# mLSTM heads with tokens on partitions: denominators as a column of the values product, norm and gate inside the heads' block

## What is computed

```python
def mlstm_mixer(h, w_in, gate_b, head_g, w_out):
    q, k, v, ig, fg, og = jnp.split(h @ w_in, splits, axis=-1)
    hh = mlstm_chunkwise(heads(q), heads(k), heads(v), i_pre, f_pre)
    hh = rmsnorm(hh.transpose(0, 2, 1, 3), head_g).reshape(B_, S, A_V_W)
    return (hh * jax.nn.sigmoid(og)) @ w_out
# inside mlstm_chunkwise, for a token t and a head:
#   s[t, u] = (q_t . k_u) * 64**-0.5 * exp(log_d[t, u] - m_t) for u <= t
#   h_t     = sum_u s[t, u] v_u / max(|sum_u s[t, u]|, exp(-m_t))
```

## Time and profile before

| | us |
|---|---|
| median of 3 runs | 3057.55 |
| lowest, highest | 3047.7, 3060.89 |
| the profiled execution, its own time | 3049.9 |
| its span in the profile | 3048.1 |
| mean granted clock of TensorE | 0.961 |
| busy: TensorE, VectorE, ScalarE, GpSimd | 2815.7, 1561.3, 871.8, 376.5 |

### The profile page before, as it was taken

How to read it: one execution, slowest core, us unless ns; L and a number is a source line. 1 busy time by engine, 2 the same in 40 slices (tenths; PEclk the granted TensorE clock), 3 DMA queues, 4 the chain that set the end, 5 groups by cost and what they waited for, 6 DMA issues and landing times. The chain is left out here.

```text
span 3048.1 us, 40943 instructions
## 1 busy us (share of the span) xinstructions
PE 2815.7 (92%) x17635; PEld 2216.8 (73%) x17635; DVE 1561.3 (51%) x2138; ACT 871.8 (29%) x1119; POOL 376.5 (12%) x356
## 2 busy tenths in 40 slices
PE   7999999788899999999999999799999669999997
PEld 6888876577765777788887854578887545688886
DVE  5555454566676734555545317463354545463342
ACT  3222234211134223322213423332222334432221
...
DMA packets 267444, 272.05 MB, mean 89 GB/s; under 512 B 12751, under 2 KB 248246, under 8 KB 267071
## 3 DMA queue, kind: packets, MB, share of 16 engines
...
## 5 line engine op out<-in xcount | busy, mean ns | idle before, releaser
L915 DVE TENSOR_TENSOR mix_wl<-ring_raw,mix_wh 128x2048 fp32r<-128x2048 f32 (+2 forms) x66 | 153.1, 2320 | 220.1 <-ACT mix_wh L807 220.0
L707 PE MATMUL mix_ps<-h_mix_hi,mix_wh 128*128 128x512 f32 x624 | 244.1, 391 | 0.0
L709 PE MATMUL mix_ps<-h_mix_lo,mix_wh 128*128 128x512 f32 x624 | 242.8, 389 | 0.0
L807 ACT ACTIVATE mix_wh<-ring_raw 128x2048 fp32r<-128x2048 f32 (+2 forms) x66 | 117.6, 1782 | 212.5 <-PE mix_ps L713 162.1
L707 PE MATMUL ffn_ps<-h_rw_hi,ffn_wh 128*128 128x512 f32 x448 | 175.3, 391 | 0.0
L709 PE MATMUL ffn_ps<-h_rw_lo,ffn_wh 128*128 128x512 f32 x448 | 174.3, 389 | 0.0
L915 DVE TENSOR_TENSOR mlp_wl<-ring_raw,mlp_wh 128x2048 fp32r<-128x2048 f32 (+1 forms) x38 | 96.7, 2545 | 131.5 <-ACT mlp_wh L807 131.5
L915 DVE TENSOR_TENSOR mlp_wl<-mlp_raw,mlp_wh 128x2048 fp32r<-128x2048 f32 x36 | 93.2, 2589 | 133.3 <-ACT mlp_wh L807 133.3
L713 PE MATMUL mix_ps<-h_mix_hi,mix_wl 128*128 128x512 f32 x624 | 154.2, 389 | 0.0
L707 PE MATMUL mlp_ps<-view,mlp_wh 128*128 128x512 f32 x384 | 150.1, 391 | 0.0
L709 PE MATMUL mlp_ps<-view,mlp_wh 128*128 128x512 f32 x384 | 149.5, 389 | 0.0
...
## 6 DMA issues: line engine op xcount, KB each, us to landing
...
```

The lines of the kernel that those rows point to most:

```text
L707: nc.tensor.matmul(ps[:, it.banks[t], :], w(h, k, t), xh[:, k, :], start=it.first and k == it.k0, stop=False)
L709: nc.tensor.matmul(ps[:, it.banks[t], :], w(h, k, t), xl[:, k, :], start=False, stop=False)
L807: nc.scalar.activation(slot(wh, it), slot(raw, it), ACT.Copy).then_inc(hi_ready, 1)
L915: nc.vector.tensor_tensor(slot(wl, it), slot(raw, it), slot(wh, it).bitcast(F32), ALU.subtract)\
```

## The change

Tokens now lie on partitions in the product with the values. The pT block (keys by queries) is the stationary operand and the values of a head are the moving one, with a column of ones behind each head's 128 values, so that the 129th column of the result is the denominator. Ten products of 129 columns a head stand for the four of `pn` and the four of `pd`; `pd`, `pe_`, the mean and `den` are gone. `v` gets a layout with 129 columns a head (`padded_heads`), and the take-out of the values product of `mix` writes into it. The floors are turned once into columns (`fcol`) by four small transposes at the start.

Per head ScalarE copies the 4 by 129 columns out (`take_head`), squares each of the four blocks with a sum (`squares`), and VectorE works on 4 columns a head (`columns`: absolute value, floor, EPS d^2, sum). Reciprocal and root are taken in three groups of heads, (0,1,2), (3,4), (5,6,7); the roots of the first two groups stand inside the loop, after the exponential of unit (4,0) and of (6,0). VectorE then scales a head (`scale`), TensorE turns it back to features on partitions by four transposes into the one bank `pt` (`turn`), and VectorE multiplies by gain and gate out of PSUM (`gate`). Heads 0 to 4 are turned in the loop, after units (4,2), (5,0), (5,2), (6,2), (7,0); heads 5 to 7 after the last unit. `head_norm_gate` is removed, and with it its barrier. Each broadcast moves one unit earlier. Ten products of `keep_clock` are added before the first unit, four ahead of the wait for the constants and six behind the first scores.

The diff, cut:

```diff
+                        if st.padded:
+                            four = st.dst[:, t, TT * it.gi:TT * (it.gi + 1), 0:P]
+                            nc.scalar.activation(four, ps[:, t, :].rearrange("p (h n) -> p h n", n=P), ACT.Copy)\
+                                .then_inc(act_out, 1)
+                        else:
+                            nc.scalar.activation(st.dst[:, t, it.gi * L:(it.gi + 1) * L], ps[:, t, :], ACT.Copy)\
+                                .then_inc(act_out, 1)
...
+def padded_heads(e, at):
+    e.views += 1
+    return e.nc.alloc_sbuf_tensor_at(f"view{e.views}", [P, TT, A_HEADS, P + 1], F32, offset=e.arena_at + at * L * 4)[:, :, :, :]
...
+MH_GROUPS = ((0, 1, 2), (3, 4), (5, 6, 7))
+MH_ROOTS = {(4, 0): 0, (6, 0): 1}
+MH_TURNS = {(4, 2): 0, (5, 0): 1, (5, 2): 2, (6, 2): 3, (7, 0): 4}
...
+    H, W = A_HEADS, P + 1
+    group_of = {h: g for g, hs in enumerate(MH_GROUPS) for h in hs}
+    left = [h for h in range(H) if h not in MH_TURNS.values()]
-        negM, floor, den = sb("negM", [P, 3, L]), sb("floor", [P, 3, L]), sb("den", [P, 2, L])
-        sq = sb("sq", [P, 2, L])
-        pm, pe_, pS, pn, pd = (pb("pm", [P, L]), pb("pe", [P, L]), pb("pS", [P, 2, L]),
-                               pb("pn", [P, 2, L]), pb("pd", [P, 2, L]))
+        negM, sq = sb("negM", [P, 2, L]), sb("sq", [P, P])
+        outT = sb("outT", [P, H, TT, W])
+        fcol, mag = sb("fcol", [P, TT, H]), sb("mag", [P, 2, TT])
+        mean, rs = sb("mean", [P, H, TT]), sb("rs", [P, H, TT])
+        pm, pS, pn, pt = pb("pm", [P, L]), pb("pS", [P, 2, L]), pb("pn", [P, 2, 2, L]), pb("pt", [P, L])
...
+        def blocks_of(h):
+            return pn[:, h % 2, :, 0:2 * W].rearrange("p b (i n) -> p b i n", n=W)
...
             def broadcast(h):
                 if h > 0:
-                    pe.wait_ge(rows_out, 2 * h)
-                nc.tensor.matmul(pm[:, :], sel[:, h, :], rows[:, 0, :], start=True, stop=True)
-                nc.tensor.matmul(pe_[:, :], sel[:, h, :], rows[:, 1, :], start=True, stop=True)\
-                    .then_inc(rows_done, 1)
-            def mean(h):
-                pe.wait_ge(squared, 2 * h + 1)
-                pe.wait_ge(abs_ready, h + 1)
-                nc.tensor.matmul(pd[:, h % 2, :], e.ones[:, :], sq[:, h % 2, :], start=True, stop=True)\
-                    .then_inc(mean_done, 1)
+                    pe.wait_ge(rows_out, h)
+                nc.tensor.matmul(pm[:, :], sel[:, h, :], rows[:, 0, :], start=True, stop=True).then_inc(rows_done, 1)
             def scores(n):
                 h, j = units[n]
@@ -2641,58 +2651,89 @@
                 nc.tensor.matmul(pS[:, n % 2, j * P:L], qk[hs, H // 2 + h // 2, j * P:(j + 1) * P],
                                  qk[hs, h // 2, j * P:L], start=True, stop=True).then_inc(s_done, 1)
+            def turn(k):
+                pe.wait_ge(scaled, k + 1)
+                if k > 0:
+                    pe.wait_ge(gated, k)
+                for i in range(TT):
+                    last = nc.tensor.transpose(pt[:, i * P:(i + 1) * P], outT[:, k, i, 0:P], e.ident[:, :])
+                last.then_inc(turned, 1)
+            for t in range(TT):
+                last = nc.tensor.transpose(pt[:, t * H:(t + 1) * H], rows[:, 1, t * P:(t + 1) * P], e.ident[0:H, 0:H])
+            last.then_inc(floors, 1)
+            keep_clock(nc, e, pn[:, 1, 1, :], 4)
             pe.wait_ge(loaded, 32)
             broadcast(0)
             scores(0)
             scores(1)
+            keep_clock(nc, e, pn[:, 1, 1, :], 6)
+            pe.wait_ge(ones_ready, 1)
+            pe.wait_ge(floors_out, 1)
             for n, (h, j) in enumerate(units):
-                if j == 1 and h + 1 < H:
+                if j == 0 and h + 1 < H:
                     broadcast(h + 1)
                 if n + 2 < len(units):
                     scores(n + 2)
-                if j == 2 and h > 0:
-                    mean(h - 1)
+                if n > 0 and units[n - 1] in MH_TURNS:
+                    turn(MH_TURNS[units[n - 1]])
                 pe.wait_ge(p_masked, n + 1)
                 if j == 0 and h >= 2:
-                    pe.wait_ge(out_done, h - 1)
-                    pe.wait_ge(squared, 2 * (h - 1))
-                first, last_j = j == 0, j == TT - 1
-                nc.tensor.matmul(pn[:, h % 2, j * P:L], v[:, j, h * P:(h + 1) * P], pT[:, n % 3, j * P:L],
-                                 start=first, stop=last_j)
-                last = nc.tensor.matmul(pd[:, h % 2, j * P:L], e.ones[:, :], pT[:, n % 3, j * P:L],
-                                        start=first, stop=last_j)
+                    pe.wait_ge(taken, h - 1)
+                for i in range(j, TT):
+                    last = nc.tensor.matmul(pn[:, h % 2, i // 2, (i % 2) * W:(i % 2 + 1) * W],
+                                            pT[:, n % 3, i * P:(i + 1) * P], v[:, j, h, :],
+                                            start=j == 0 and i % 2 == 0, stop=j == i and i % 2 == 1)
                 last.then_inc(used, 1)
-            mean(H - 1)
+            for k in left:
+                turn(k)
         @block.scalar
         def _(act):
             def take_rows(h):
                 act.wait_ge(rows_done, h + 1)
-                if h >= 3:
-                    act.wait_ge(out_done, h - 2)
-                nc.scalar.activation(negM[:, h % 3, :], pm[:, :], ACT.Copy).then_inc(rows_out, 1)
-                nc.scalar.activation(floor[:, h % 3, :], pe_[:, :], ACT.Copy).then_inc(rows_out, 1)
-            def take_sum(h):
+                if h >= 2:
+                    act.wait_ge(arg_ready, TT * (h - 1))
+                nc.scalar.activation(negM[:, h % 2, :], pm[:, :], ACT.Copy).then_inc(rows_out, 1)
+            def take_head(h):
                 act.wait_ge(used, TT * (h + 1))
-                if h >= 2:
-                    act.wait_ge(out_done, h - 1)
-                nc.scalar.activation(den[:, h % 2, :], pd[:, h % 2, :], ACT.Abs).then_inc(abs_ready, 1)
-                nc.scalar.activation(sq[:, h % 2, :], pn[:, h % 2, :], ACT.Square).then_inc(squared, 1)
-                nc.scalar.activation(out[:, h, :], pn[:, h % 2, :], ACT.Copy).then_inc(squared, 1)
+                nc.scalar.activation(outT[:, h, :, :].rearrange("p (b i) n -> p b i n", b=2), blocks_of(h), ACT.Copy)\
+                    .then_inc(taken, 1)
+            def squares(h):
+                act.wait_ge(taken, h + 1)
+                for i in range(TT):
+                    if TT * h + i > 0:
+                        act.wait_ge(squared, TT * h + i)
+                    nc.scalar.activation(sq[:, :], outT[:, h, i, 0:P], ACT.Square, accum_out=mean[:, h, i:i + 1])\
+                        .then_inc(squared, 1)
+            def root(g):
+                hs = MH_GROUPS[g]
+                act.wait_ge(inv_ready, g + 1)
+                part = rs[:, hs[0]:hs[-1] + 1, :]
+                nc.scalar.activation(part, part, ACT.Sqrt).then_inc(rs_ready, 1)
+            act.wait_ge(floors, 1)
+            nc.scalar.activation(fcol[:, :, :], pt[:, 0:TT * H].rearrange("p (t h) -> p t h", h=H), ACT.Copy)\
+                .then_inc(floors_out, 1)
             take_rows(0)
             for n, (h, j) in enumerate(units):
                 act.wait_ge(arg_ready, n + 1)
                 nc.scalar.activation(dT[:, n % 3, j * P:L], dT[:, n % 3, j * P:L], ACT.Exp).then_inc(d_ready, 1)
-                if j == 0 and h > 0:
-                    take_sum(h - 1)
+                if j == 1 and h > 0:
+                    take_head(h - 1)
                 if j == 2 and h + 1 < H:
                     take_rows(h + 1)
-            take_sum(H - 1)
+                if j == 2 and h > 0:
+                    squares(h - 1)
+                if (h, j) in MH_ROOTS:
+                    root(MH_ROOTS[h, j])
+            take_head(H - 1)
+            squares(H - 1)
+            root(len(MH_GROUPS) - 1)
-            def floored(h):
-                d = den[:, h % 2, :]
-                dve.wait_ge(abs_ready, h + 1)
-                then(nc.vector.tensor_tensor(d, d, floor[:, h % 3, :], ALU.max))
-                st.mark(nc.vector.scalar_tensor_tensor(d, d, EPS, d, ALU.mult, ALU.mult))
-            def finish(h):
-                dve.wait_ge(steps, st.n)
-                dve.wait_ge(mean_done, h + 1)
-                nc.vector.scalar_tensor_tensor(inv[:, h, :], pd[:, h % 2, :], 1.0 / P, den[:, h % 2, :],
-                                               ALU.mult, ALU.add).then_inc(out_done, 1)
-            def invert(h, j):
-                part = inv[:, h, j * P:(j + 1) * P]
-                dve.wait_ge(out_done, h + 1)
-                nc.vector.reciprocal(part, part)
+            def columns(h):
+                d, m, c = outT[:, h, :, P], mag[:, h % 2, :], rs[:, h, :]
+                dve.wait_ge(taken, h + 1)
+                then(nc.vector.scalar_tensor_tensor(m, d, -1.0, d, ALU.mult, ALU.max))
+                then(nc.vector.tensor_tensor(m, m, fcol[:, :, h], ALU.max))
```

(49 more changed lines are left out.)

51 lines of the change are left out of this document (13 added, 38 removed).

## The result

| | before | after |
|---|---|---|
| median, us | 3055.85 | 3015.52 |
| lowest, highest | 3047.7, 3060.89 | 3013.11, 3019.93 |
| the profiled execution | 3049.9 | 3013.11 |
| its span | 3048.1 | 3011.3 |
| mean granted clock | 0.961 | 0.962 |

The medians are of four runs each. The ratio is 0.9869, with a 95% interval of 0.9851 to 0.9887: the change is 1.3% faster. The page answers the earlier trace rows with this line.

A forecast was written before the change was run, and what follows sets the result against it. TensorE, at a clock not always full, bounds the loop; a VectorE, ScalarE and GpSimd chain bounds the last 24.0 us. Loop -32.9, start -1.7, tail -14.0 sum to -48.6: 3001 by the profile, 3005 with half the offset; range 2990 to 3033.

The forecast's parts named there:

- The price of a values product: Loop: ten 129-column products a head at 0.225 us each, 2.35 taken, making a head 6.27 us; other bound 3.2.
- five turns: Loop: five heads turned back by four transposes each, 2.5 us in all added on TensorE.
- the gates: Loop: gates on VectorE wait for turns and delay the next pT, 0.4 us each, 2.0 in all.
- the roots: Loop: two roots with table loads ahead of exponentials, 1.5 us of 2.8 each, 3.0 in all.
- The rule of the Trainium skill that was weighed: Table switches cost 2.66 us: in-loop roots 2.8 more each, tail 1.4 more, sum near -42 in place of -48.6.
- 18.5% on the loop: Loop: lower clock costs the same ratio as before, turning 53.3 us into 63.2 against 96.1, -32.9.
- The start: Up to the first values product: one broadcast fewer on the path, -1.7 us; +4.2 if at the lower clock.
- at 1804.4: Start: six keep_clock products of some 0.47 us end here if the upper clock holds; first values product at 1805.9.
- The tail: After the last values product: 10.0 us in place of 24.0, -14.0; single-bank turns 6 and 7 wait 1.4 each.
- The chain of ScalarE and VectorE: Loop rival: 4.6 and 4.7 us of chained work set the head at 8.3 us; 3021, chance 0.19.
- The lower clock throughout: Loop rival: clock low all through, small products overlapped, a head 12.5 us; 3045 in all, chance 0.10.
- The slower case: Loop rival: each small product pays its weight load at the lower clock, a head 15.7 us; +18, 3072, chance 0.04.

The follow-up runs named there:

- fifth experiment: The changed kernel, keep_clock products included, with the broadcast's operands zero-padded from 8 to 128 rows: 3004.95 us, ratio 0.9840 to the kernel before.
- third: The changed kernel with values products of 128 columns in place of 129, the column of ones left out: 3018.1 us, ratio 0.9875 to the kernel before.
- sixth: The changed kernel with 128-column values products, no keep_clock, and weights and moving operand of these products exchanged: 3002.64 us, ratio 0.9819 to the kernel before.
- ninth experiment: The changed kernel without keep_clock, all values products of a unit written to one region of PSUM: 3010.11 us in one run.
- twelfth experiment: The kernel before the change with both its broadcasts a head padded to 128 rows: 3041.04 us, ratio 0.9965 to the kernel before.
- eleventh: The changed kernel with all roots, turns, scales and gates behind the loop, keep_clock kept, and the broadcast on 128 rows: 3006.89 us, ratio 0.985 to the kernel before.
- last combination: The changed kernel with 128-row broadcast, later gates, tail turns in three banks, unchained squares, and only the first four keep_clock products: 2990.49 us, ratio 0.9791.
- second experiment: The changed kernel with all roots, turns, scales and gates moved behind the loop: 3025.92 us, ratio 0.9897 to the kernel before.
- first experiment: The changed kernel without its ten keep_clock products at the start of the heads' block: 3002.25 us, ratio 0.9816 to the kernel before.
- eighth: The changed kernel without keep_clock, with gates two units after their scale, tail turns in three banks and unchained squares: 3004.3 us, ratio 0.982 to the kernel before.

## Why the prediction was right, point by point

It was right in sign, in mechanism and within its range: 3005 predicted, 3015.5 measured. The block gave 41.0 us of the 48.6 expected; of the 7.6 that were missing the loop has 4.6, the start 2.1 and the tail 0.8.

**The price of a values product: the step that was mis-sized.** "Ten give 2.3; the other bound is the 128-column product of this stage, half of 0.64, 3.2 for ten. I take 2.35." Measured: 3.02 a head, near the bound that wasn't taken, and a head of 7.00 us in place of 6.27. Over eight heads that is 5.8 us, more than the 4.6 that the loop gave less; the clock gave a part back. An estimate from the fifth experiment's loop, 57.4 us, with 0.19 a head put back for the broadcast, is 58.9 us at the upper clock where the sum had 53.3, and so 8.8 for the clock where it had 9.9. Part of the price is how the runs are cut: a run of one takes 0.41 and each further product 0.22 to 0.24 (0.65 - 0.41, 0.87 - 0.65, 1.09 - 0.87). With that, the further product costs what the attention stage has, 0.225, and each of the four runs pays some 0.18 on top, 0.7 a head. The prediction priced runs of 4, 3, 2 and 1 by the mean over a stream. In the attention stage the run of four starts 0.90 before the next form, so this toll isn't paid there. Width, operand roles and place in PSUM don't explain it (third, sixth and ninth experiment).

What goes with it is the number of rows of the neighbours in TensorE's stream. By the rows below, a product of 128 rows costs some 0.09 to 0.10 us more for each neighbour of 64 or 8 rows. A run of one 128-column product between neighbours of 128 rows costs 0.22 in the attention stage (transposes ahead of it, scores of 128 rows behind):

```profile
2548.46 0.39 PE L3030 MATMUL at_po<-at_pT,view 128*128 128x128 f32 x2
2548.68 0.39 PE L3010 MATMUL at_pS<-view,view 128*128 128x128 f32 x2
```

With one such neighbour it costs 0.33 (behind scores of 64 rows, ahead of the 128-row broadcast, fifth experiment), with two 0.41 (ahead of the 8-row one, after). The twelfth experiment changed the broadcasts' rows alone in this place, and 0.95 and 0.96 became 0.86 for a product of 512 columns on either side of the change. The kernel before had paid the same: its pair of 128-column products between two scores took 0.64, as the run of two does here with 0.65. So "half of 0.64" was two further products with two tolls, and the price of ten products depends on how many runs they make: by these rows ten times 0.225 and four times two tolls, 3.0 a head. For the broadcast this rests on an experiment. For the scores it fits the distances of the heads' block, but their rows weren't varied; in the attention stage a run of two between 128-row neighbours takes 0.55 (from 2540.67), 0.10 more than it gives. What the engine does at such a change stays open.

**Turns, gates and roots.** The fifth experiment and the eleventh, both wholly at the upper clock, give these without the clock: loops of 57.4 and 50.4 us. Of the 7.0 between them, five turns are some 2.6, as predicted (TensorE's busy time, 52.77 - 50.13), and TensorE's idle time is 4.3 (57.40 - 52.77, less 0.3), where 2.0 for the gates and 3.0 for the roots had been predicted. The sum was close, but its parts were not: of the seven idle stretches in the fifth experiment four (0.36, 0.50, 0.36 and 1.22) end with a pT that stood on VectorE behind a gate, one (0.55) with a pT behind the columns and a scale, and two (1.04 and 0.56) with the mask on GpSimd at the loop's end, the first of them behind a pT that had stood behind a gate too. The table loads cost next to none: the last combination, with both roots in its loop, has TensorE idle for 0.9 us of it in all (53.10 - 52.24), and after, TensorE was full from 1834 to 1838 while ScalarE did this (its timeline):

```profile
1833.85 1.28 ACT L2717 ACT_TABLE_LOAD   x1
1835.14 0.21 ACT L2717 ACTIVATE mh_rs<-mh_rs 128x12 f32<-128x12 f32 x1
1835.37 1.28 ACT L2725 ACT_TABLE_LOAD   x1
1836.66 0.52 ACT L2725 ACTIVATE mh_dT<-mh_dT 128x384 f32<-128x384 f32 x1
```

The rule of the Trainium skill that was weighed ("ScalarE: Activation LUTs", section "What ACT_TABLE_LOAD costs") didn't hold here: the root starts 1.29 us after its load starts, and the Exp 1.29 after the next, so there is no room for the drain of 1.38 that the page adds to each. The Trainium skill's advice, in the same page's section on table sets, is to do all functions of one set first. Here that puts scales, turns and gates behind the loop as well. The second experiment's tail was 13.0 us longer by it; net of what the loop gains, the block took 85.2 us (eleventh experiment) against 78.9 (fifth), both without a fall in the loop. The prediction was right to go by the row.

**The clock.** The prediction put 18.5% on the loop, 9.9 us, because before had it. After, 25.5 us of the loop ran at the lower level. The distances between a head's copy and the next give its price: the last four are 11.50, 12.33, 9.00 and 8.26, in the first experiment 7.17, 9.41, 7.44 and 7.47, 9.6 us less for the same work. The size was right, but it was luck: other orders of nearly the same work gave 4 to 52 us of low clock, the ninth experiment moved it from 4.2 to 22.7 with TensorE's order unchanged, and with the spread broadcast there was none.

**The start.** Predicted -1.7, measured +0.4. The step that failed is "at 1804.4": six keep_clock products at 0.47. They took 4.47 us, as part of them ran at the lower clock, on the path. The prediction had named that case, with about 5 us and +4.2; the truth lay between. Where its condition held, its number nearly did: in the second experiment, with the start as in the change and all of it at the upper clock, the six take 2.8 us and the start 10.6, -1.4. Without any of them the start takes 9.5 us, with the four under the wait alone 8.8.

**The tail.** Predicted 10.0, measured 10.9. The squares came 0.43 apart (predicted 0.5), and the first turn waited 4.67 for the last root and scale. The two turns behind it each waited for a gate in the single bank, as predicted, but at the lower clock a turn took 1.08 from start to end, where the sum had 0.7 with its handoffs, so they came 2.0 apart and not 1.4. With three banks the tail is 8.2.

**The rivals.** The chain of ScalarE and VectorE doesn't set the head: TensorE is full for all of the 7.00 us, with VectorE busy for 3.96 and ScalarE for 4.24. ScalarE had been put a little too high, at 4.6. VectorE had been put too low: its 4.7 counts 1.4 for a scale and a gate, which this head hasn't, so 3.3 stand against 3.96. The slip is in the working, where 7.97 less about 6 is 2.0 and not 2.5, and pT with the arguments takes more than either. Heads with a turn were the tight ones, as the waits above show. The lower clock throughout didn't come in the change as it is; the third experiment had it for 52.5 of 79.8 us and the eighth for 42.4 of 73.5. The slower case, weights loaded in the open at the lower clock, didn't come: in the 17.1 us at 0.50, 17.10 of PE stand over 10.79 of PEld, in heads of 11.5 and 12.3, not 15.7. The Trainium skill's rule on transposes and the clock ("TensorE: Matmul & The Clock Gate", section "Part 4: PE-mode transpose") played no part: the last combination has five turns in its loop and a granted clock of 1.00.
